# A two-model kernel for one core: the depthwise convolution shared with VectorE, remainders of weights and retention's products later, norm gains ahead of the root

## What is computed

```
# first block, per layer (a = rmsnorm(h))
u = a @ w_in            # q, k, v, index queries and keys, conv part, pool part
idx = sum_h relu(qi_h @ ki^T) * wi_h ; keep the 64 largest per token
y_attn = softmax(q @ k^T / 8, only kept keys) @ v          # 8 heads
y_conv = silu(layernorm(depthwise31(conv part) + b)) @ pw  # 256 channels, 31 taps
y_pool = (window sums / count - x) @ pool_w * pool_scale
h += rmsnorm([y_attn, y_conv, y_pool] @ w_out)
h += rmsnorm(relu(rmsnorm(h) @ w_up)^2 @ w_down)
h += sigmoid(h @ ple_gate) * (p @ ple_proj)
# second block, per layer
x += 0.5 * rmsnorm(swiglu(rmsnorm(x)))
x += rmsnorm(mixer(rmsnorm(x)))   # linear recurrence, retention of 4 heads, short conv, gates
x += 0.5 * rmsnorm(swiglu(rmsnorm(x)))
```

## Time and profile before

| | |
|---|---|
| median of 3 runs | 2494.39 us (2494.33 to 2498.67) |
| the profiled execution | 2500.17 us |
| its span, first to last instruction | 2498.4 us |
| TensorE matmuls busy | 2408.8 us (96%), x12668 |
| VectorE busy | 1524.3 us (61%) |
| ScalarE busy | 1169.3 us (47%) |
| GpSimd busy | 133.2 us (5%) |
| mean granted TensorE clock | 0.984 |
| a chunk's load, issue to landing | 4.8 us (median) |
| `masked` of one head, VectorE | 0.56 + 0.61 us, 1.3 with the hand-overs |
| `squares_o`, two squares with their sums, ScalarE | 1.3 us |

### The profile page before, as it was taken

How to read it: one execution, slowest core, us unless ns; L and a number is a source line. 1 busy time by engine, 2 the same in 40 slices (tenths; PEclk the granted TensorE clock), 3 DMA queues, 4 the chain that set the end, 5 groups by cost and what they waited for, 6 DMA issues and landing times.

```text
span 2498.4 us, 30422 instructions
## 1 busy us (share of the span) xinstructions
PE 2408.8 (96%) x12668; PEld 2049.9 (82%) x12668; DVE 1524.3 (61%) x1661; ACT 1169.3 (47%) x1378; POOL 133.2 (5%) x255
## 2 busy tenths in 40 slices
PE   7989998999998999999999999999999999999998
PEld 6878877878887887888888888888879788887887
DVE  6656565656656655775575555565567755755654
ACT  5434344444444544545444444444445454444543
POOL 0500000500000000000000000000000000000000
PEclk9999999999999999999999999999999999999999
DMA  7215544214453554543555445545545336554453
GB/s 259 90 68 185 213 170 185 101 68 185 182 184 140 221 190 163 202 164 136 204 185 200 150 171 187 184 184 188 190 166 208 140 137 217 185 202 152 161 186 134
DMA packets 61624, 427.07 MB, mean 171 GB/s; under 512 B 7088, under 2 KB 7344, under 8 KB 11568
## 3 DMA queue, kind: packets, MB, share of 16 engines
q1 hardware_dynamic: 61488, 425.13, 46.6%
HBM read 424.05 MB, written 1.05 MB: 170 GB/s over the span
## 4 chain that ended last, share of the span: by engine, by line
PE 84%; DVE 7%; ACT 4%; DMA 2%; POOL 1%; issue 1%; DVEq 0%; SPq 0%; ACTq 0%; POOLq 0%
PE ub L1480 24%; PE ub L1481 12%; PE ub L1463 7%; PE ub L1465 7%; PE ub L1464 7%; PE acc L1463 6%; PE acc L1465 6%; PE acc L1464 6%; DVE wlo L881 3%; ACT whi L479 3%; PE acc L1744 2%; DMA raw<-in_w 2%; ACT junk L501 1%; DVE XN L913 1%; PE acc L1521 1%
## 5 line engine op out<-in xcount | busy, mean ns | idle before, releaser
L881 DVE TENSOR_TENSOR wlo<-raw,whi 128x2048 fp32r<-128x2048 f32 x388 | 888.6, 2291 | 393.4 <-ACT whi L479 392.8
L1480 PE MATMUL ub<-xhl,whi 128*128 128x512 f32 (+1 forms) x2752 | 941.8, 394 | 11.3 <-DVE xhl L919 11.3
L479 ACT ACTIVATE whi<-raw 128x2048 fp32r<-128x2048 f32 x388 | 741.5, 1911 | 253.3 <-DMA raw<-in_w 110.8
L1481 PE MATMUL ub<-xhl,wlo 128*128 128x256 f32 (+1 forms) x2752 | 755.7, 275 | 0.0
L1480 PEld LDWEIGHTS ub<-xhl,whi 128*128 128x128 f32 x2752 | 527.8, 192 | 121.5 <-DVE wlo L881 13.1
L1481 PEld LDWEIGHTS ub<-xhl,wlo 128*128 128x128 f32 x2752 | 531.2, 193 | 2.4
L1463 PE MATMUL acc<-whi,bhl 128*128 128x512 f32 x736 | 289.7, 394 | 3.8 <-DVE bhl L1261 3.1
L1465 PE MATMUL acc<-whi,bhl 128*128 128x512 f32 x736 | 287.1, 390 | 0.0
L1464 PE MATMUL acc<-wlo,bhl 128*128 128x512 f32 x736 | 286.9, 390 | 0.0
L1463 PE MATMUL ub<-whi,xhl 128*128 128x512 f32 (+1 forms) x512 | 202.4, 395 | 14.8 <-DVE wlo L881 8.1
L1464 PE MATMUL ub<-wlo,xhl 128*128 128x512 f32 (+1 forms) x512 | 199.0, 389 | 0.0
(11 more groups left out here) (298 smaller groups left out, 2758.5 us busy)
## 6 DMA issues: line engine op xcount, KB each, us to landing
raw<-in_w SPq DMA_DIRECT2D x388, 1024.0 KB, 4.8
gain<-in_gains SPq DMA_DIRECT2D x20, 512.0 KB, 6.5
par<-in_par SPq DMA_DIRECT2D x2, 1068.0 KB, 7.0
DEC<-in_decay SPq DMA_DIRECT2D x2, 768.0 KB, 6.2
H<-in_x SPq DMA_DIRECT2D x2, 512.0 KB, 5.5
out_h<-H SPq DMA_DIRECT2D x4, 256.0 KB, 2.2
par<-in_par SPq DMA_DIRECT2D x2, 419.0 KB, 7.6
PT<-in_p SPq DMA_DIRECT2D x2, 256.0 KB, 7.8
```

The source lines that it names most:

```text
L479: do(act.activation(whi[:, s % RING, :], raw[:, s % RAW, :], ACT.Copy), counts["w_hi"])
L881: do(dve.tensor_tensor(wlo[:, s % RING, :], raw[:, s % RAW, :], whi[:, s % RING, :].bitcast(f32), ALU.subtract), counts["w_lo"])
L1480: pe.matmul(both, w_h, x[:, :, c], start=first, stop=False, skip_group_check=True)
L1481: return pe.matmul(both[:, 1, :], w_l, x[:, 0, c], start=False, stop=last, skip_group_check=True)
```

## The change

Five things are changed, and no product with a weight is.

- The convolution. Of the second group's 31 taps the last 16 (`TAPS_DVE`) go to VectorE: `own_taps` multiplies the shifted input by a per-channel weight and adds it up in a new tile `CD`, four taps in each of heads 0 to 3. TensorE adds `CD` with one matmul by the identity, after its own 46 taps, which now stand 14 ahead of the heads (31 before) and 7, 7, 6, 6, 6 within heads 0 to 4. GpSimd makes 30 diagonals, then the pool part, then 16 more. The layer norm behind the convolution is moved: each step of it stands one or two heads later, and the last matmuls of it stand within the output product (`last_values`, `made`).
- Remainders of weights. VectorE's `lo` of three chunks moves from the rounds of the top-k and from ahead of the heads into the heads. In the norms ahead of a product that begins feature-major (two chunks by halves), VectorE makes no remainder for t = 1 until `lo_x(1)` is done. The same is done ahead of the gate product (`sp_`), where the remainder of chunk `sp_ + 3` now stands behind `lo_x(1)`.
- The norm. `post` multiplies the product by its gain as soon as it is squared, and the root comes in with the addition to H.
- The last chunk of a `tail` is taken column half by column half, not row unit by row unit.
- Retention: `scores2(0)` stands behind g's first chunk, `values(hd)` behind the second chunk of a head, not the first, and what follows is moved with it.

```diff
-TAPS_BEFORE, TAPS_AFTER = 31, (8, 8, 8, 7)
+TAPS_DVE = 16
+TAPS_BEFORE, TAPS_AFTER = 14, (7, 7, 6, 6, 6)
...
-                    early = TAPS + TAP_RING
+                    early = TAP_RING + TAPS_BEFORE
                     tap_diagonals(0, early)
...
-                    tap_diagonals(early, 2 * TAPS)
+                    tap_diagonals(early, 2 * TAPS - TAPS_DVE)
...
                             if j % 2 == 0:
                                 if hd:
                                     turned_p(hd - 1)
-                                squares_o(hd)
                             else:
                                 used(s)
                                 for t in range(2):
                                     do(act.activation(tS[:, t, :], ub[:, 2 * (hd % 2) + t, :], ACT.Silu),
                                        counts["sg_ready"])
+                                squares_o(hd)
...
-                    nxt("ry")
                     settle()
                     for fb in range(2):
-                        do(dve.scalar_tensor_tensor(tX[:, fb, :], acc[:, bank(t, fb), :], ry[:, t:t + 1],
-                                                    gain[:, 0, fcol(fb)], ALU.mult, ALU.mult), counts["y_free"])
+                        nxt("ssy")
+                        do(dve.tensor_tensor(tX[:, fb, :], acc[:, bank(t, fb), :], gain[:, 0, fcol(fb)], ALU.mult),
+                           counts["y_free"])
+                    nxt("ry")
                     for fb in range(2):
                         dve.wait_ge(sem["y_free"], counts["y_free"].n - 1 + fb)
-                        do(dve.tensor_tensor(H[:, t, fcol(fb)], H[:, t, fcol(fb)], tX[:, fb, :], ALU.add),
-                           counts["h_ready"])
+                        do(dve.scalar_tensor_tensor(H[:, t, fcol(fb)], tX[:, fb, :], ry[:, t:t + 1], H[:, t, fcol(fb)],
+                                                    ALU.mult, ALU.add), counts["h_ready"])
...
+                    def own_taps(first, end):
+
+                        for k in range(first, end):
+                            w = par1[:, P1["dw"] + TAPS + k:P1["dw"] + TAPS + k + 1]
+                            y = YC[:, 1, k:k + S]
+                            settle()
+                            if k == TAPS - TAPS_DVE:
+                                do(dve.tensor_scalar(CD[:, 0, :], y, w, None, ALU.mult))
+                            else:
+                                do(dve.scalar_tensor_tensor(CD[:, 0, :], y, w, CD[:, 0, :], ALU.mult, ALU.add),
+                                   counts["cd_ready"] if k == TAPS - 1 else None)
+
                     masked(0)
                     masked(1)
-                    lo(s0 + 14)
+                    lo(s0 + 12)
+                    dve.wait_ge(sem["par_in"], 16 * (L + 1))
                     for hh in range(HEADS):
                         if hh + 2 < HEADS:
                             masked(hh + 2)
+                        if hh < 4:
+                            if hh in (1, 3):
+                                lo(s0 + 13 + hh // 2)
+                            k0 = TAPS - TAPS_DVE + 4 * hh
+                            own_taps(k0, k0 + 4)
...
                         post(t, acc_bank)
-                        lo(sf + 2 * t)
+                        if t == 0:
+                            lo(sf)
                         pre(t, XN1)
-                        if t:
-                            lo(sf + 3)
                         lo_x(t)
-                        lo(sf + 2 * t + 1)
+                        lo(sf + 1 + 2 * t)
...
                         post(t, acc_bank)
                         lo(sp_ + 2 * t)
-                        if t:
-                            lo(sp_ + 3)
                         lo_x(t)
                         lo(sp_ + 2 * t + 1)
                     lo(sg + 3)
...
                         if hh == 4:
+                            nxt("cd_ready")
+                            give(pe.matmul(acc[:, 3, S:2 * S], ident, CD[:, 0, :], start=False, stop=True), "conv_done")
...
-                            if (kind, j) == ("k", 3):
-                                scores2(0)
                         elif kind == "g":
                             hd = j // 2
                             block_of(s, j, hd % 2, "sg_ready", xhi, xlo)
-                            if j % 2 == 0:
-                                if hd:
-                                    turn_p(hd - 1)
+                            if j == 0:
+                                scores2(0)
+                            elif j % 2 == 0:
+                                turn_p(hd - 1)
+                            else:
                                 values(hd)
                                 if hd + 1 < RET_HEADS:
                                     scores2(hd + 1)
```

More of the change, by code:

```diff
@@ L650, in _ @@
                         turned(hh)
+                        if hh == 6:
+                            nxt("ha_ready")
+                            do(act.activation(tS[:, 0, :], two(cacc, 0), ACT.Square), counts["sq_ready"])
+                    attended(1)
                     nxt("ha_ready")
@@ L1193, in _ @@
                                counts["h_ready"])
-                        lo(sg + 4 + 2 * t)
+                        if not (t and L + 1 == LAYERS):
+                            lo(sg + 4 + 2 * t)
                         pre(t, XN1)
-                        if t:
+                        if t and L + 1 < LAYERS:
                             lo(sg + 7)
@@ L1223, in ffn, with norms @@
                         return s0 + 32
-                    def norms(end, more=True):
+                    def norms(end, more=True, blocks=False):
                         for t in range(2):
                             post(t, acc_bank)
-                            lo(end + 1 + 2 * t)
+                            if blocks or t == 0:
+                                lo(end + 1 + 2 * t)
                             if more:
                                 pre(t, XN2)
-                            if t:
+                            if blocks and t:
                                 lo(end + 4)
@@ L1299, in weighed @@
                                    counts["mixed"] if final and t else None)
-                    norms(ffn("f1"))
+                    norms(ffn("f1"), blocks=True)
                     sv = s2(L, "v", 0)
@@ L1501, in columns @@
                         arrive(s)
-                        for k in range(2):
+                        order = [(k, fb) for k in range(2) for fb in range(2)]
+                        if c == n - 1 and ends:
+                            order = [(k, fb) for fb in range(2) for k in range(2)]
+                        for k, fb in order:
                             u = unit_of(2 * c + k)
-                            if ready:
+                            if ready and fb == 0:
                                 ready(2 * c + k)
-                            for fb in range(2):
-                                final = (c, k) == (n - 1, 1)
-                                last = wide_tile(banks(t, fb), bhi[:, u, cols(t)], blo[:, u, cols(t)], s,
-                                                 k * D + fb * 512, fresh and (c, k) == (0, 0), final and ends > 0)
-                                if final and fb < ends:
-                                    give(last, "half_done")
+                            final = (c, k) == (n - 1, 1)
+                            last = wide_tile(banks(t, fb), bhi[:, u, cols(t)], blo[:, u, cols(t)], s,
+                                             k * D + fb * 512, fresh and (c, k) == (0, 0), final and ends > 0)
+                            if final and fb < ends:
+                                give(last, "half_done")
                         if free:
@@ L1765, in _ @@
                             give(last, "mean_done")
-                        if hh == 5:
-                            nxt("sq_ready")
-                            fill(A_[3], "var_ready")
-                            for k in range(2):
-                                last = pe.matmul(acc[:, 3, 0:S], means[:, :], tS[:, 0, k * S:(k + 1) * S], start=k == 0, stop=k == 1)
-                            give(last, "stat_done")
-                            turn_values(0)
                         if hh == 6:
```

110 lines of the change are left out of this document (59 added, 51 removed).

## The result

The changed kernel takes 2452.45 us in the median of 4 runs (2449.33 to 2455.83), the kernel before 2494.9 on the same chip (2494.33 to 2498.67). The ratio is 0.983, with a 95% interval of 0.981 to 0.984: 42 us faster, where 41.2 were forecast. The profiled execution took 2455.83 us, its span is 2454.0, 44.4 less than before.

What follows compares the result with a forecast made beforehand. TensorE, its matmuls busy for 96% of the span, was taken to bound the kernel. Terms -9.4 - 26.7 + 6.6 - 2.2 - 8.2 - 1.3 = -41.2 us, from 2494.4 to 2453; range 2438 to 2472.

Steps and rivals of the forecast that it cites:

- Term 1: Attention, two layers: fewer TensorE taps and no layer-norm wait, less a new wait for GpSimd's diagonal; -4.7 us a layer, -9.4.
- some seven taps at 0.45: Attention: GpSimd, on its way through diagonals and pool part, is held by about seven VectorE taps, 0.45 us each.
- the slack that the forecast had given VectorE: Attention: VectorE's taps, remainders and masking need 20.5 us, to 117.8; TensorE comes for CD at 121.3.
- Term 2: Five norms ahead of a two-chunk start: TensorE starts t = 1 2.65 us sooner, plus 2.7 of clock each; -26.7 us.
- that load doesn't move: Five norms: the load under ScalarE's copy ahead of `hi_x` begins at an unmoved remainder and ends at 1437.65 as before.
- I expect the drop in one of four: Five norms: with waits of 2.0 us instead of 3.7, the half clock follows in one of four.
- For the clock I had 13.5: Five norms: half-clock stretches cost 3.3 us each on average, 0.6 is left, so 2.7 gained in each of five.
- Term 3: Gate product, twice: TensorE waits 4.0 us as the third chunk's remainder stands behind `lo_x(1)`; a loss of 3.3 each, +6.6.
- Terms 4, 5, 6: Other norms, -2.2 us; retention, twice, without the wait for k, -8.2; the end, one pair of operations gone, -1.3.
- GpSimd isn't held up, or catches up: Rival for attention: GpSimd isn't held up, or catches up in the gaps, giving -19.0 there and 2443.6 us; chance 0.15.

Runs made afterwards that it cites:

- experiment 6: Changed kernel with the weight remainder of head 1 moved to head 2: 2448.1 us, ratio 0.980 to the kernel before.
- experiment 4: Changed kernel with the remainder of the gate product's fourth chunk ahead of `lo_x(1)` again: 2448.4 us, ratio 0.981 to the kernel before.
- experiment 5: Changed kernel with ScalarE's `hi_x(1)` ahead of its copy of the third chunk in norms before a two-chunk start: 2444.9 us, ratio 0.979 to the kernel before.
- 8: Changed kernel with the edits of experiment 4, experiment 5 and experiment 6 together: 2434.6 us, ratio 0.975 to the kernel before.
- 11: Kernel of experiment 8 with ScalarE's squares for t = 0 ahead of the chunk copy and VectorE's XN ahead of its remainder: 2418.5 us, ratio 0.969.
- 2: Kernel before with the norms' edits alone (`post`, later remainders, gate product's order, last chunk by column halves): 2476.9 us, ratio 0.991.
- 7: Changed kernel with VectorE's 16 taps in heads 2 and 3, eight each, out of the pool part: 2449.5 us, one execution.
- 10: Changed kernel with the last chunk of a tail taken row unit by row unit again: 2453.7 us, ratio 0.982 to the kernel before.
- 3: Kernel before with retention's new order alone: 2486.4 us, ratio 0.996.
- 9: Kernel before with the gain ahead of the root and the last chunk by column halves, no remainder moved: 2490.0 us, ratio 0.998.

## Why the prediction was right in the sum and wrong in two terms

**Term 1, attention: -9.4 forecast, -16.6 measured. The step that failed is "some seven taps at 0.45".** The forecast let GpSimd wait for every tap of VectorE, 3.2 us in all, put the first diagonal behind the pool part at 113.8, and took 3.4 us of wait and 1.4 of half clock from that. It came at 110.3, TensorE came to it at 109.1, so the wait was 1.2 us, and the clock stayed at full. The whole trace is 1.4 us early from the program's start; without that TensorE came on time and the diagonal 2.1 us sooner than forecast. 6.6 (matmuls) + 1.9 (the layer norm's wait) + 1.0 (its half clock, taken as forecast, up to 1.7) - 1.2 is 8.3 a layer, which is what the trace shows.

What the remainders cost GpSimd was about right: 1.1 and 2.3 us forecast, 2.2 (the diagonal at 95.98, 2.52 us for 0.37) and 1.9 seen, and moving the second (experiment 6) takes the wait away. The taps' price was put on the wrong engine. GpSimd's instructions in the pool part last 0.7 to 1.3 us and follow each other 0.08 us apart, so a tap nearly always finds one running, and it ends behind it. The eight taps there took 3 us more than alone, out of the slack that the forecast had given VectorE, and cost GpSimd 0.4 us instead of 3.2. CD was still done at 119.6, ahead of TensorE at 121.6.
The Trainium skill (SBUF - State Buffer, Who interferes with whom) says that the issue order, not the shape of the operation, decides who blocks. In the pool part the trace agrees: the tap of 108.66 to 110.03 took 1.37 us behind a GpSimd instruction of 108.42 to 109.75, which took 1.33 (1.27 alone). To the hundredth the recorded starts don't show it: the diagonal of 95.98 and the remainder of 95.98 begin together, and it is the diagonal that is drawn out. I had read the rule for one side only.

**Term 2, the five norms: -26.7 forecast, -20.3 measured. The steps that were off are "that load doesn't move", by 1.9 us in one norm, and "I expect the drop in one of four".** Take the time from TensorE's wait for XN of t = 0 to its start of t = 1. It was 17.6 us in each of the five before, and the forecast takes 2.65 off, which leaves 14.9. Measured were 15.1, 14.9, 14.8, 14.7 and 16.8, in the order of the program. So the chain was forecast to 0.2 us where the load was on time, and ScalarE's copy, which waits for the load, is what sets the start, as the forecast had it. In the last norm the load took 6.8 us and not 4.8. The forecast had taken its length as fixed, and it stands on the path with nothing to spare. In all, the starts come 11.5 us sooner, where 13.3 had been forecast.
For the clock I had 13.5, which left less than a fifth of what it had cost. The half-clock stretches in the five sum to 44.4 us before and 13.7 after. Counting only what TensorE did at the half clock from its start of t = 1 on (the work ahead of it is in the 11.5), half of that is 16.2 us lost before and 6.8 after, 9.4 gained. (With the 11.5 that is some 21; the comparison by places gives 20.3.) The drop came in three of five, one of them the late load's, where one of four had been forecast.

**Term 3: +6.6 forecast, +6.3 in the traces, 4 us between the medians** of experiment 4 and the changed kernel. The step, VectorE standing before `lo_x(1)` with the needed remainder behind it, is seen in experiment 4's rows.

**Terms 4, 5, 6** came as forecast, each within 0.5 us. Head 0's and head 3's waits in retention are 0.74 and 0.82, forecast 0.6 and 1.1; the scores, now behind g's first chunk, run at full clock.

That the total was right to 1 us in the median (to 3 in the two traces) is luck: term 1 was 7 too small and term 2 was 6 too large, for reasons that have nothing to do with each other. The range, made of the rivals, covered either alone. The rival "GpSimd isn't held up, or catches up", given 0.15, is nearest to what happened in attention (-19.0 against -16.6).

Open: how much of the clock's gain is the change's and how much is luck of one execution. The table below shows why it can't be read off one trace.

## What to carry to other kernels

When one engine has to make the next product's operand and also a weight chunk's copy, ask of each such copy whether its load has landed: an in-order engine that stands for a late load holds everything queued behind it. Putting the short step of the chain (squares, `hi_x`) first cost nothing here, as no new wait for weights appeared, and gave 24 us (7.6 in experiment 5, 16 between 8 and 11) on top of the change's 42. And when two engines exclude each other, price both sides: the long instruction makes the other wait, whichever engine it is on.

## What the runs showed of the hardware

The start of t = 1 behind eight short transposes is the same stretch of work in every kernel, with waits of differing length, in the profiled executions of the changed kernel and of experiments 2, 4 to 8, 10 and 11:

| TensorE's wait at the start of t = 1 | starts | followed by the half clock |
|---|---|---|
| 0.84 us | 15 | 0 |
| 1.13 to 1.40 us | 14 | 4 |
| 1.42 to 3.33 us | 16 | 14 |

The stretches behind these starts are 3.4 or 6.8 us long, so a wait that grows by half a microsecond can cost 1.7 to 3.4 us on top. The same wait needn't give the same clock: TensorE waits 1.9 us for the layer norm of the convolution in the kernel before and in experiments 2, 3 and 9, and the half clock follows in 5 of the 8 places.

A load of 1 MB that takes 4.8 us in the median took 6.8 at the same place in another layer of one execution. That is not rare: 19 of the 388 loads of that execution took more than 6 us, some of them with another load still under way.

GpSimd's diagonals, 0.37 us alone, took 0.54 beside VectorE's taps and 2.5 beside a remainder of 2.28. A tap, 0.48 alone and beside a diagonal, took 1.37 beside a GpSimd instruction of 1.33. So it is the shorter instruction that pays in each of these pairs.
